# The second block's input units as three fp32r products each, with their split halves made on ScalarE and VectorE and one expert transfer issued later

## The chip, the cores and the metric

The program runs on one core of one Trainium2 chip. The metric is the device time of one execution in microseconds (us), the median of the runs shown. The core has TensorE (PE, with its weight loads as PEld), VectorE (DVE), ScalarE (ACT), GpSimd (POOL) and SyncE (SP, which here only issues transfers). "Granted clock" is the share of TensorE's full clock in a stretch.

## What is computed

The reference is two models in a row on 256 tokens of width 1024, all in fp32. The first block has two layers (three mixing branches and a feed-forward part); the second block has one layer with modulation from a vector c, differential attention with four heads, a pooling branch, and 32 experts of which each token uses two. Around the change only these lines matter:

```python
mod = jax.nn.silu(c) @ w_ada[l] + b_ada[l]
sh1, sc1, g1, sh2, sc2, g2 = jnp.split(mod, N_MOD, axis=-1)
h = rms_norm(x, norm1_g[l]) * (1.0 + sc1[:, None]) + sh1[:, None]
z = h @ w_in[l]
...
x = x + g1[:, None] * mix
...
y = hierarchical_moe(h, w_rg, b_rg, w_re, b_re, w_gate, w_up, w_down)
```

The changed part is `z = h @ w_in`: 1024 inputs to 2048 columns (query, key, value and pool input, 512 each).

## The kernel before

**Units and the ring.** All weights come from HBM as one stream of units of 1 MB (128 partitions x 2048 fp32). SP issues them in the order of the stream into a ring of four slots; unit n waits until unit n - 4 is done on PE (L868 to L870). A unit of w_in holds 256 output columns: eight chunks of 128 inputs. `gemm2` (L1352) multiplies it with `u`, the modulated input (eight chunks of 128 x 256), in 32 fp32 products of 128 x 128 by 128 x 256, into one of two banks, which ACT copies out (`win_read`, L2122).

**Split products.** The rest of the kernel multiplies large matrices as three fp32r products: ACT writes the high part of a unit (a copy to fp32r, L2064), DVE the low part (unit minus high part, L2735, in place in the ring), the input has a high and a low part too, and PE adds high x high, high x low and low x high (L1064, L1069). The eight input units of the second block are the exception: they are multiplied as they are.

**Order in the second block.** The order of each engine's work is written out by hand. Units in the stream are numbered from the block's start: 0 and 1 are the first pair of modulation units, the eight input units lie at 2, 3, 6, 7, 10, 13, 14, 15 (`WIN_AT`), pairs of modulation units between them, 20 to 23 are the output units, 24 is the router, and then 192 units of experts follow. On PE (L1472 to L1511): norms, the first pair, `win(0)`, `win(2)`, a turn for rope, a pair, `win(4)`, a turn for rope, `win(6)`, a pair, the values' turn, scores of head 0, `win(7)`, scores of head 1, a pair, `win(1)`, turn of the weights of head 0, a turn for rope, `win(3)`, values of head 0, turn of the weights of head 1, a turn for rope, `win(5)`. In the text these eight are units 1 to 8 in this order. After them come the rest of attention and pooling, two pairs, the output products (`out_products`, L1452), the router, and the experts.

On DVE the same stretch runs: `both_norms` (L2753, writes u; ACT's `modulate2`, L2099, then scales it chunk by chunk in place), `first_norm` (L2760, rescales h), the keeping of modulation columns, two rope steps (L2837, three instructions that wait for PE's turn), values, maxima and weights of head 0, maxima of head 1, `pool_means` (L2807), copy of the turned weights of head 0, a rope step, weights of head 1, its copy, a rope step. An engine takes its instructions in this order, and a wait holds up all behind it.

**Expert transfers ahead of time.** Expert units 0 to 21 have places of their own, and SP issues them between the ring's units as their places come free (L871 to L902). Units 2 to 6 go behind the ring units 5 to 9 (L875); unit 7, whose place is u, waits for the last input unit (L878). Later expert units need a place that an earlier one gave up: the next is issued when the first expert's first unit is done on PE (L904). The experts' products then run per expert: gate and up (L1674), turns, down (L1708), with transfers of two units at once.

## Time and profile before

| | us |
|---|---|
| runs before | 2069.06, 2069.35, 2070.88 |
| median | 2069.35 |
| the profiled execution | 2068.3 |
| its span (first to last instruction) | 2066.5 |
| PE busy | 1930.7 (93%) |
| DVE busy | 1265.8 (61%) |
| ACT busy | 923.8 (45%) |
| DMA queue of SP | 479.57 MB, 60.2% of 16 engines' span |

All times below are microseconds from the span's start of this execution, whose own time is 2068.3; the median of the runs is 1.05 more. The second block starts near 1486, its input units run from 1493 to 1565, and the experts from 1629 to the end. A busy PE is not PE at its peak: products overlap in the records. A line can be that of a helper that many places call.

### The profile page before, as it was taken

What the parts mean: (1) busy time and instruction counts of PE and PEld (TensorE: products, weight loads), DVE (VectorE), ACT (ScalarE), POOL (GpSimd) and SP (SyncE); (2) the same over time, 40 slices, a digit from 0 to 9 for tenths busy, and PEclk for the clock granted to TensorE, in tenths of its full rate; (3) what the DMA queues carried; (4) which work ended last, traced back from release to release, by engine and by line L of the source; (5) the groups of instructions that cost most, each with busy time, mean ns of one, the idle gap of its engine ahead of it and who ended that gap; (6) DMA issues with size and microseconds to landing.
All of it is one profiled execution on the core that took longest, in us unless ns stands there. A gap on an engine that the chain in (4) does not pass through costs nothing.

```text
span 2066.5 us, 46188 instructions
## 1 busy us (share of the span) xinstructions
PE 1930.7 (93%) x19900; PEld 1726.2 (84%) x19900; DVE 1265.8 (61%) x2069; ACT 923.8 (45%) x1100; POOL 31.4 (2%) x62
## 2 busy tenths in 40 slices
PE   8999999999999999999999999999999897777766
PEld 7998989999999999989899999999987664454444
DVE  6889887698787468898885896885543311111111
ACT  5555644674555455557365755554412210111101
POOL 0000000000000000000000000000000000000000
PEclk9999999999999999999999999999999998899898
DMA  6455434545455554554544454455787899999997
GB/s 242 175 214 184 182 147 163 204 144 187 181 184 191 193 184 174 199 210 157 183 154 172 176 184 165 183 184 199 277 328 282 344 428 428 428 428 429 428 429 313
DMA packets 60272, 498.92 MB, mean 241 GB/s; under 512 B 7152, under 2 KB 7280, under 8 KB 12240
## 3 DMA queue, kind: packets, MB, share of 16 engines
q1 hardware_dynamic: 54864, 479.57, 60.2%
q0 software_dynamic: 4384, 14.49, 2.1%
q8 instruction: 129, 2.11, 0.4%
q10 hardware_dynamic: 864, 2.49, 0.3%
q14 instruction: 31, 0.25, 0.0%
HBM read 495.38 MB, written 1.15 MB: 240 GB/s over the span
## 4 chain that ended last, share of the span: by engine, by line
PE 77%; DMA 17%; DVE 4%; ACT 1%; issue 1%; ACTq 0%; SPq 0%; DVEq 0%
PE bank L1064 34%; PE bank L1069 17%; DMA arena<-stream 15%; PE bank L1009 4%; PE bank L1674 3%; PE bank L1361 3%; PE bank L1052 2%; DMA ring<-stream 1%; PE bank L1057 1%; DVE ring_r L2735 1%; PE banks_by_token L1267 1%; PE banks_by_token L1236 1%; PE bank L1708 1%; PE bank L1653 1%; PE bank L1106 1%
## 5 line engine op out<-in xcount | busy, mean ns | idle before, releaser
L1069 PE MATMUL bank<-gh_and_scan_weights_high,ring_r 128*128 128x256 f32 x2368 | 308.3, 283 | 0.7 <-DVE ring_r L2735 0.7
L2735 DVE TENSOR_TENSOR ring_r<-ring,weights_and_u_split 128x2048 fp32r<-128x2048 f32 x108 | 247.1, 2289 | 85.4 <-ACT weights_and_u_split L2064 81.8
L1069 PEld LDWEIGHTS bank<-gh_and_scan_weights_high,ring_r 128*128 128x128 f32 x2368 | 294.8, 192 | 1.1 <-DVE ring_r L2735 1.1
L2064 ACT ACTIVATE weights_and_u_split<-ring 128x2048 fp32r<-128x2048 f32 x108 | 205.8, 1908 | 83.3 <-PE bank L1069 53.5
L3096 DVE COPY arena<-bank 128x128 f32<-128x128 f32 x32 | 9.3, 292 | 288.8 <-PE bank L1692 288.8
L1674 PE MATMUL bank<-arena 128*32 128x256 f32 x1504 | 109.7, 443 | 60.7 <-DMA arena<-stream 59.8
L2735 DVE TENSOR_TENSOR ring_r<-ring,hidden_and_weights_high 128x2048 fp32r<-128x2048 f32 x64 | 146.1, 2286 | 32.9 <-ACT hidden_and_weights_high L2064 32.8
L2248 ACT ACTIVATE arena<-bank 64x256 f32<-64x256 f32 x32 | 12.1, 378 | 318.0 <-PE bank L1674 318.0
L1674 PEld LDWEIGHTS bank<-arena 128*32 128x32 f32 x1504 | 54.8, 124 | 111.6 <-issue 52.3
L1064 PE MATMUL bank<-gh_and_scan_weights_high,weights_and_u_split 128*128 128x256 f32 x992 | 141.1, 285 | 1.6 <-ACT weights_and_u_split L2064 1.6
L2307 DVE SCALAR_TENSOR_TENSOR arena<-bank,par,arena 128x255 f32<-128x255 f32 (+1 forms) x272 | 111.3, 475 | 48.8 <-ACT arena L1857 48.6
L1064 PEld LDWEIGHTS bank<-gh_and_scan_weights_high,weights_and_u_split 128*128 128x128 f32 x992 | 127.8, 192 | 3.3 <-ACT weights_and_u_split L2064 2.0
L1868 ACT ACTIVATE arena<-bank 128x512 f32<-128x512 f32 x96 | 56.9, 595 | 160.9 <-PE bank L1069 158.0
L2064 ACT ACTIVATE hidden_and_weights_high<-ring 128x2048 fp32r<-128x2048 f32 x64 | 122.0, 1908 | 9.8 <-PE bank L1009 8.5
L1064 PE MATMUL bank<-gh_and_scan_weights_high,hidden_and_weights_high 128*128 128x256 f32 x864 | 123.6, 286 | 0.0
L1064 PE MATMUL bank<-u_r,weights_and_u_split 128*128 128x256 f32 x864 | 121.3, 283 | 0.0
L1064 PE MATMUL bank<-u_r,hidden_and_weights_high 128*128 128x256 f32 x864 | 121.3, 283 | 0.0
L1857 ACT ACTIVATE arena<-bank,par 128x256 f32<-128x256 f32 x112 | 57.1, 561 | 130.3 <-PE bank L1069 127.6
L1064 PEld LDWEIGHTS bank<-gh_and_scan_weights_high,hidden_and_weights_high 128*128 128x128 f32 x864 | 111.2, 191 | 4.9 <-issue 4.3
L1064 PEld LDWEIGHTS bank<-u_r,weights_and_u_split 128*128 128x128 f32 x864 | 111.5, 192 | 0.0
L1064 PEld LDWEIGHTS bank<-u_r,hidden_and_weights_high 128*128 128x128 f32 x864 | 111.4, 192 | 0.0
L1064 PE MATMUL bank<-hidden_low,weights_and_u_split 128*128 128x256 f32 x608 | 86.0, 283 | 0.0
(497 smaller groups left out, 3493.8 us busy)
## 6 DMA issues: line engine op xcount, KB each, us to landing
ring<-stream SPq DMA_DIRECT2D x267, 1024.0 KB, 4.8
arena<-stream SPq DMA_DIRECT2D x55, 2048.0 KB, 25.8
ring<-stream SPq DMA_DIRECT2D x26, 2048.0 KB, 26.7
arena<-stream SPq DMA_DIRECT2D x19, 1024.0 KB, 9.8
arena<-rows_scratch POOLq DMA_DIRECT2D x48, 256.0 KB, 4.2
place_of_rows<-stream SPq DMA_DIRECT2D x2, 1024.0 KB, 6.4
place_of_parameters<-stream SPq DMA_DIRECT2D x2, 1024.0 KB, 6.5
h<-x_d ACTq DMA_DIRECT2D x4, 256.0 KB, 4.6
```

The source lines that it names most:

```text
L1009: mm = pe.matmul(G[use % GBANKS][:, :], xx[:, 4 * late + k, i * P:(i + 1) * P], wx[:, k, :], start=(not late and part == k == 0), stop=(la ...
L1052: pe.matmul(bank[:, c * S:(c + 1) * S], ww[k][:, c * P:(c + 1) * P], yhi[k] if xhi is None else xhi[:, k, :], start=(c == part == k == 0), ...
L1057: mm = pe.matmul(bank[:, c * S:(c + 1) * S], whi[k][:, c * P:(c + 1) * P], xlo[:, k, :], start=False, stop=(k == KC - 1), skip_group_check ...
L1064: pe.matmul(bank[:, c * S:(c + 1) * S], whi[k][:, c * P:(c + 1) * P], yhi[k] if xx is None else xx[:, k, :], start=(sub == 0 and c == part ...
L1069: mm = pe.matmul(bank[:, c * S:(c + 1) * S], wlo[k][:, c * P:(c + 1) * P], yhi[k] if xhi is None else xhi[:, k, :], start=False, stop=(end ...
L1361: mm = pe.matmul(G[b][:, c * S:(c + 1) * S], w[:, k, c * P:(c + 1) * P], x[:, k, :], start=(k == 0), stop=(k == KC - 1))
L1674: mm = pe.matmul(G[0][g:g + 32, 0:S], xe[:, 2 * j + k, a * SLOTS:(a + 1) * SLOTS], w[k][:, g * 8:g * 8 + S], start=(j == k == 0), stop=(j ...
L1857: a = act.activation(arena[:, dst, :], bank[:, c * S:(c + 1) * S], ACT.Identity, scale=pc(wn, ch * width + width // 2), bias=pc(bn, ch))
L1868: act.activation(flat(at, 2), bank[:, :], func).then_inc(f.sem, 1)
L2064: act.activation(high(k), scan_high_or_low(k, ring[:, POS[k] % RING, :]), ACT.Copy).then_inc(whi_ok.sem, 1)
L2307: ins = stt(o, bank[:, c * S + lo + d:c * S + hi + d], pc(wn, chans[c] * width + j), o, ALU.mult, ALU.add)
L2735: tt(scan_high_or_low(k, ring_r[:, POS[k] % RING, :]), scan_high_or_low(k, w), high(k).bitcast(F32), ALU.subtract)\
```

## The change

Each of the eight input units becomes three passes of 16 fp32r products: high part of the unit x high part of u, low part x high part of u, high part x low part of u. Below, these passes are the first, middle and last third of a unit. The first third waits for ACT's high part, the middle third for DVE's low part, the last third of the first unit in effect for the low part of u. ACT writes the high parts (`win_high`) into two places in turn, 138 and 88; DVE makes the low parts in place in the ring (`win_low`), the high part of u in eight casts and its low part in one subtraction (`u_parts`). Place 88 was expert unit 5's, so that transfer is issued behind the last input unit, ahead of expert unit 7.

```diff
@@ SP
                 elif second and 5 <= early < E_EARLY + 3:
                     sp.wait_ge(h_new.sem, h_new.at(DEPTH, 0))
-                    expert_unit(early - 3)
+                    if early - 3 != 5:
+                        expert_unit(early - 3)
                 elif second and early == WIN_AT[-1] + RING:
                     sp.wait_ge(*done2(WIN_AT[-1]))
+                    expert_unit(5)
                     expert_unit(7)
@@ PE
-            def gemm2(m, x):
+            def gemm2(m):
                 b, before = use2(m)
-                pe.wait_ge(*landed2(m))
+                n = WIN_AT.index(m)
+                whi, wlo = (x.rearrange("p (k m) -> p k m", k=KC) for x in (flat_r(WIN_HI[n % 2], KC), ring_r[:, m % RING, :]))
+                pe.wait_ge(whi_ok.sem, whi_ok.at(DEPTH, n + 1))
                 pe.wait_ge(freed[b].sem, before)
...
+                for part, (w, x) in enumerate(((whi, chunks_r(UHI, KC)), (wlo, chunks_r(UHI, KC)), (whi, u_r))):
+                    if part == 1:
+                        pe.wait_ge(wlo_ok.sem, wlo_ok.at(DEPTH, n + 1))
+                    elif part == 2:
+                        pe.wait_ge(ulo_ok.sem, ulo_ok.at(DEPTH, 1))
+                    for c in range(2):
+                        for k in range(KC):
+                            if part == n == c == 0:
+                                pe.wait_ge(uhi_ok.sem, uhi_ok.at(DEPTH, k + 1))
...
@@ ACT
+            def win_high(n):
+                m = WIN_AT[n]
+                act.wait_ge(*landed2(m))
+                if n >= 2:
+                    act.wait_ge(*done2(WIN_AT[n - 2]))
+                act.activation(flat_r(WIN_HI[n % 2], KC), ring[:, m % RING, :], ACT.Copy).then_inc(whi_ok.sem, 1)
...
             norm2(1)
+            win_high(0)
             modulate2()
...
+            act.wait_ge(h_new.sem, h_new.at(DEPTH, 0))
+            win_high(1)
             win_read(0)
             win_read(2)
+            win_high(2)
             ada_read2(1)
+            win_high(3)
...
             win_read(7)
+            win_high(5)
...
@@ DVE
+            def u_parts():
+
+                for c in range(KC):
+                    dve.wait_ge(u_ready.sem, u_ready.at(DEPTH, c + 1))
+                    V.tensor_copy(flat_r(UHI + c, 1), u[:, c, :]).then_inc(uhi_ok.sem, 1)
+                win_low(0)
+                dve.wait_ge(uhi_ok.sem, uhi_ok.at(DEPTH, KC))
+                tt(u_r[:].rearrange("p c s -> p (c s)"), u[:].rearrange("p c s -> p (c s)"), flat_r(UHI, KC).bitcast(F32), ALU.subtract)\
+                    .then_inc(ulo_ok.sem, 1)
+
+            def win_low(n):
+
+                m = WIN_AT[n]
+                dve.wait_ge(whi_ok.sem, whi_ok.at(DEPTH, n + 1))
+                tt(ring_r[:, m % RING, :], ring[:, m % RING, :], flat_r(WIN_HI[n % 2], KC).bitcast(F32), ALU.subtract).then_inc(wlo_ok.sem, 1)
...
             both_norms()
+            u_parts()
             first_norm()
...
+            win_low(1)
...
             rope(0, 0)
+            win_low(2)
             rope(2, 1)
+            win_low(3)
             ada_keep2(1)
+            win_low(4)
             values_kept(0)
...
             ada_keep2(2)
+            win_low(5)
             maxima(1)
             pool_means()
             ada_keep2(3)
+            win_low(6)
             turned(0)
             rope(1, 2)
+            win_low(7)
             weights(1)
```

DVE from the writing of u to the second rope step, before (arena is the large working area, banks_by_token the banks that PE's turns go to):

```order
L2757 TENSOR_TENSOR u<-arena,rstd 128x512 x4
L2764 SCALAR_TENSOR_TENSOR h<-arena,rstd 128x256 x8
...
L2787 TENSOR_TENSOR mod<-bank,arena 128x4
...
L2843 TENSOR_TENSOR arena<-banks_by_token,arena 128x512
L2844 TENSOR_TENSOR arena<-arena 128x512
L2846 TENSOR_TENSOR arena<-arena 128x512
L2843 TENSOR_TENSOR arena<-banks_by_token,arena 128x512
```

And the same stretch in the changed kernel (L2799 is a low part, L2792 the low part of u):

```order
L2782 TENSOR_TENSOR u<-arena,rstd 128x512 x4
L2789 CAST u_high_and_scan_weights_high<-u 128x256 x8
L2799 TENSOR_TENSOR ring_r<-ring,u_high_and_scan_weights_high 128x2048
L2792 TENSOR_TENSOR u_r<-u,u_high_and_scan_weights_high 128x2048
L2805 SCALAR_TENSOR_TENSOR h<-arena,rstd 128x256 x8
...
L2828 TENSOR_TENSOR mod<-bank,arena 128x4
L2799 TENSOR_TENSOR ring_r<-ring,weights_and_u_split 128x2048
...
L2885 TENSOR_TENSOR arena<-banks_by_token,arena 128x512
L2886 TENSOR_TENSOR arena<-arena 128x512
L2888 TENSOR_TENSOR arena<-arena 128x512
L2799 TENSOR_TENSOR ring_r<-ring,u_high_and_scan_weights_high 128x2048
L2885 TENSOR_TENSOR arena<-banks_by_token,arena 128x512
```

The final norm of h now stands behind the casts and two subtractions, and between two rope steps stands the low part of a unit. Later on DVE, behind the pooling (its last two instructions are the first rows here), the changed kernel has:

```order
L2860 TENSOR_TENSOR arena<-arena 128x256
L2862 TENSOR_TENSOR arena<-arena 128x256
L2828 TENSOR_TENSOR mod<-bank,arena 128x4
L2799 TENSOR_TENSOR ring_r<-ring,u_high_and_scan_weights_high 128x2048
L2932 COPY arena<-bank 128x512
L2885 TENSOR_TENSOR arena<-banks_by_token,arena 128x512
L2886 TENSOR_TENSOR arena<-arena 128x512
L2888 TENSOR_TENSOR arena<-arena 128x512
L2799 TENSOR_TENSOR ring_r<-ring,weights_and_u_split 128x2048
L2915 RECIPROCAL small<-small 128x4
```

Two low parts stand between the pooling and the weights of head 1 (which begin with the reciprocal); before, the same rows stood there without the two L2799. On SP, from the seventh ring unit's neighbours to the output units, before:

```order
L870 DMA ring<-stream 128x2048
L866 DMA arena<-stream 128x2048
L870 DMA ring<-stream 128x2048
L866 DMA arena<-stream 128x2048
L870 DMA ring<-stream 128x2048 x10
L866 DMA u<-stream 128x2048
L870 DMA ring<-stream 128x2048 x4
```

and in the changed kernel (arena and u here are the places of expert units):

```order
L871 DMA ring<-stream 128x2048 x2
L867 DMA arena<-stream 128x2048
L871 DMA ring<-stream 128x2048 x10
L867 DMA arena<-stream 128x2048
L867 DMA u<-stream 128x2048
L871 DMA ring<-stream 128x2048 x4
```

One transfer to the arena moved from the early stretch to the place between the last two of the input block's ring transfers and the four output units, ahead of the transfer to u.

## Rows read from the trace of the kernel before

**Rows 1.** Chain of waits near the end: start us, us, what

```profile
1692.88 26.70 DMA arena<-stream
...
2015.38 27.25 DMA arena<-stream
```

**Rows 2.** The page's moved bytes, 40 equal slices of the span

```profile
GB/s 242 175 214 184 182 147 163 204 144 187 181 184 191 193 184 174 199 210 157 183 154 172 176 184 165 183 184 199 277 328 282 344 428 428 428 428 429 428 429 313
```

**Rows 3.** Five-us stretches: length, PE, PEld, DVE, ACT, POOL busy, PEclk, DMA, GB/s

```profile
1590.00:1595.00 5.00, 3.63 (x17) 3.22 (x18) 0.00 (x0) 4.13 (x6) 0.00 (x0) 1.00 0.99 416
...
1620.00:1625.00 5.00, 2.56 (x119) 2.37 (x122) 3.89 (x25) 2.52 (x6) 0.00 (x0) 0.78 0.93 351
1625.00:1630.00 5.00, 3.01 (x97) 2.43 (x92) 0.73 (x4) 2.97 (x9) 0.00 (x0) 0.84 0.11 46
```

**Rows 4.** Timeline of SP's issues: start us, us, queue, line, transfer

```profile
1565.60 0.43 SPq L866 DMA_DIRECT2D u<-stream  x1
...
1630.91 0.33 SPq L866 DMA_DIRECT2D place_of_rows<-stream  x1
```

**Rows 5.** Chain of waits through the input units (L1361) to the output units

```profile
1478.38 1.92 PE bank L1069 x16
...
1493.65 7.10 PE bank L1361 x32
...
1508.23 0.86 PE banks_by_token L1391 x4
...
1558.29 6.91 PE bank L1361 x32
...
1570.59 5.73 DMA ring<-stream
```

**Rows 6.** Page, costliest groups: busy us, mean ns of one, idle before and releaser

```profile
L2735 DVE TENSOR_TENSOR ring_r<-ring,weights_and_u_split 128x2048 fp32r<-128x2048 f32 x108 | 247.1, 2289 | 85.4 <-ACT weights_and_u_split L2064 81.8
...
L2064 ACT ACTIVATE weights_and_u_split<-ring 128x2048 fp32r<-128x2048 f32 x108 | 205.8, 1908 | 83.3 <-PE bank L1069 53.5
```

**Rows 7.** DVE's groups by line and form, one copy in SBUF

```profile
L2639 DVE COPY arena<-arena 128x512 f32<-128x512 f32 x8 | 3.1, 424 | 0.1
```

**Rows 8.** Timeline of ACT and DVE: start us, us, engine, line, operation

```profile
1490.53 0.42 ACT L2090 ACTIVATE rstd<-rstd 128x256 f32<-128x256 f32 x1
...
1491.71 4.04 ACT L2103 ACTIVATE u<-u,mod 128x256 f32<-128x256 f32 x8 [0.76 <-DVE u L2757]
...
1497.07 3.25 DVE L2764 SCALAR_TENSOR_TENSOR h<-arena,rstd 128x256 f32<-128x256 f32 x8 [3.59 <-ACT rstd L1878]
...
1509.13 0.69 DVE L2843 TENSOR_TENSOR arena<-banks_by_token,arena 128x512 f32<-128x512 f32 x1 [7.62 <-PE banks_by_token L1391]
...
1510.45 0.69 DVE L2846 TENSOR_TENSOR arena<-arena 128x512 f32<-128x512 f32 x1
...
1537.04 0.60 ACT L2126 ACTIVATE arena<-bank 128x512 f32<-128x512 f32 x1 [3.63 <-PE bank L1361]
...
1538.48 1.29 DVE L2860 TENSOR_REDUCE small<-banks_by_token 128x2 f32<-128x512 f32 x2 [0.87 <-PE banks_by_token L1413]
...
1539.88 0.69 DVE L2811 COPY arena<-arena 128x1024 f32<-128x1024 f32 x1
...
1547.01 0.42 DVE L2820 TENSOR_TENSOR arena<-arena 128x256 f32<-128x256 f32 x1
...
1548.38 0.69 DVE L2890 COPY arena<-bank 128x512 f32<-128x512 f32 x1 [0.39 <-PE bank L1426]
...
1551.30 0.18 DVE L2873 RECIPROCAL small<-small 128x4 f32<-128x4 f32 x1
...
1552.43 0.88 DVE L2882 SCALAR_TENSOR_TENSOR arena<-arena,small 128x256 f32<-128x256 f32 x2
```

**Rows 9.** DMA issues at 1565 to 1566: target, KB, us to landing

```profile
ring<-stream SPq DMA_DIRECT2D x1, 1024.0 KB, 4.7
u<-stream SPq DMA_DIRECT2D x1, 1024.0 KB, 6.9
```

More of the change, by code:

```diff
@@ L347, in program @@
         HALF_AT = 120
+        WIN_HI = (138, 88)
         def bank(i):
@@ L1350, in first_norm @@
                 mm.then_inc(ss_ready.sem, 1)
-            def gemm2(m, x):
+            def gemm2(m):
                 b, before = use2(m)
-                pe.wait_ge(*landed2(m))
+                n = WIN_AT.index(m)
+                whi, wlo = (x.rearrange("p (k m) -> p k m", k=KC) for x in (flat_r(WIN_HI[n % 2], KC), ring_r[:, m % RING, :]))
+                pe.wait_ge(whi_ok.sem, whi_ok.at(DEPTH, n + 1))
                 pe.wait_ge(freed[b].sem, before)
-                w = ring[:, m % RING, :].rearrange("p (k m) -> p k m", k=KC)
-                for c in range(2):
-                    for k in range(KC):
-                        if m == WIN_AT[0] and c == 0:
-                            pe.wait_ge(u_ready.sem, u_ready.at(DEPTH, k + 1))
-                        mm = pe.matmul(G[b][:, c * S:(c + 1) * S], w[:, k, c * P:(c + 1) * P], x[:, k, :],
-                                       start=(k == 0), stop=(k == KC - 1))
+                for part, (w, x) in enumerate(((whi, chunks_r(UHI, KC)), (wlo, chunks_r(UHI, KC)), (whi, u_r))):
[7 more added lines that the diff above has]
+                                pe.wait_ge(uhi_ok.sem, uhi_ok.at(DEPTH, k + 1))
+                            mm = pe.matmul(G[b][:, c * S:(c + 1) * S], w[:, k, c * P:(c + 1) * P], x[:, k, :],
+                                           start=(part == c == k == 0), stop=(part == 2 and k == KC - 1), skip_group_check=True)
                 mm.then_inc(unit_done.sem, 1)
@@ L1382, in win @@
             def win(j):
-                gemm2(win_unit(j), u)
+                gemm2(win_unit(j))
             def rope_turn(j):
@@ L2150, in _ @@
                 return
+            act.wait_ge(h_new.sem, h_new.at(DEPTH, 0))
+            win_high(1)
             win_read(0)
             win_read(2)
+            win_high(2)
             ada_read2(1)
+            win_high(3)
             win_read(4)
             win_read(6)
+            win_high(4)
             ada_read2(2)
@@ L2158, in _ @@
             win_read(7)
+            win_high(5)
             ada_read2(3)
             exps(1)
+            win_high(6)
             win_read(1)
+            win_high(7)
             win_read(3)
```

## The prediction

> **What bounds the kernel now.** I read the end first. In the chain of waits the last 350 us are mostly one kind of step, a transfer of two expert units of 26 to 27 us, with a few microseconds of products between [rows 1]; the page's line of moved bytes stands at 428 GB/s there [rows 2]. So the last part is bound by bytes, and its length is fixed once it runs. The second question is what starts it. By the table of short stretches DMA is nearly idle at 1625 to 1630 (0.11) [rows 3], and SP issues its next transfer at 1630.91 [rows 4]. That transfer waits for the first expert's first unit on PE: every other place is full. So whatever makes the first expert start later or earlier by x moves the end by x. Earlier, that is capped at the 6 us or so of this lull; later, there is no cap. The third view is the chain from 1493 to 1577 [rows 5]: the eight input units, the turns and small steps between them follow each other on PE without a wait. The last unit ends at 1565.20, and at 1570.59 the chain changes to the transfer of the first output unit, which lands at 1576.3. From there PE, ACT and PE again lead to the first expert. I therefore ask two things: when does the eighth unit end, and when does that output unit land?
>
> **What the change saves on PE.** A unit is 32 fp32 products, 7.10 us (6.91 for the last two) [rows 5]. Sixteen fp32r products of the same size take 1.92 us [rows 5], so 48 take 5.76: 1.34 us saved a unit (1.15 for the last two), 10.3 us in all if PE waits for nothing.
>
> **What it adds.** ACT gets eight high parts of 1.908 us, DVE eight low parts of 2.289 us [rows 6], DVE also eight casts of one chunk of u and a subtraction of all of u. For the cast no row exists; a copy of 512 columns takes 0.424 us [rows 7], so 256 lie between half and all of that, and I take 0.3: it is paced by ACT anyway, and only the last one shows. The subtraction has the size of a low part, 2.29. DVE and ACT take their instructions in order, and the order decides which of these are hidden. PE needs a unit's low part for its middle third, 1.92 us after the unit starts.
>
> *Unit 1.* ACT is free at 1490.95 [rows 8] and now first makes the high part, to 1492.86. The eight modulations (4.04) [rows 8] end at 1496.9 instead of 1495.75. The last cast ends near 1497.3, the low part at 1499.6, the low part of u at 1501.95, and only then comes PE's last third, to 1503.9. Before, the unit ended at 1500.75 [rows 5]: **3.1 later**, though the products are fewer.
>
> *Units 2 to 4.* DVE now does the 3.25 us of the final norm of h [rows 8] behind these: 1501.95 to 1505.2. Small steps reach 1505.6, the low part 1507.9. PE has done the first third of unit 2 by then and waits about 1.8 us; the other two thirds (3.84) end at 1511.75. Now a loop closes. DVE's next instructions are a rope step, which waits for PE's turn after unit 2, and the low part of unit 3 stands behind it. Turn 0.86 [rows 5], rope 2.0 (1509.13 to 1511.14) [rows 8], low part 2.29, two thirds 3.84: 9.0, with hand-overs 9.1. So unit 3 ends at 1520.85, and unit 4, behind the second rope step, at 1529.95. DVE's idle time during a unit, which could have hidden these low parts, lies on the wrong side of the rope step.
>
> *Units 5 and 6.* Some 3.5 us of other PE work, unchanged, stand ahead of unit 5, and its low part is ready in time: the unit takes its 5.76 and ends at 1539.25. Unit 6 doesn't wait either. Here 1.34 each is gained.
>
> *Units 7 and 8.* From the end of unit 5 DVE is the chain. ACT reads the bank (0.60) [rows 8] and makes the sixth high part, to 1541.8; DVE does its low part, to 1544.1, the maxima (1.4 from their start to the next step), to 1545.5, and the pooling of 7.55 us (1539.88 to 1547.43) [rows 8], to 1553.1. Then low part 2.29, copy 0.69, rope 2.0, low part 2.29, weights 2.0 (1551.30 to 1553.31) [rows 8]: 1562.4, with hand-overs 1562.5. PE waits some 2.7 us in unit 7 for the first of these low parts, and 2.2 us ahead of the turn of the second head's weights, which stands before unit 8. After that two turns (1.3) and 5.76: unit 8 ends at **1569.6, 4.4 later** than 1565.20. Overlaps of neighbouring DVE instructions could take 0.6 off this, the delay of each wake-up could add 0.5.
>
> *The moved transfer.* Expert unit 5 (1 MB) leaves a stretch in which no unit waits for its weights and now stands, with unit 7 behind it, ahead of the first output unit. Before, unit 7's transfer was issued at 1565.60 [rows 4] and landed 6.9 us later [rows 9], at 1572.5; the output unit was issued at 1570.59 and landed at 1576.3 [rows 5], 3.8 after it. So it already lay behind a transfer, and one more 1 MB at 428 GB/s [rows 2] is 2.45 us: the upper end. A landing without a queue takes 4.7 us [rows 9], so 1.0 of the output unit's 5.73 was queue or disturbance, and the queue could have had up to 1.35 us of room: at least 2.45 - 1.35 = 1.1 must show. I take **2.1**, near the upper end, as the transfers ran almost without a gap. PE has no other work to put there. SP itself issues the same number of transfers; its order else is unchanged, and POOL's queue is not touched.
>
> **The sum.** 4.4 + 2.1 = 6.5 us. Nothing behind takes it up: from 1576 to the first expert each step waits for the one before, the transfers there are issued by that chain, and the byte-bound rest starts with it. The profiled execution (2068.3, span 2066.5) would give 2074.8; the median of the runs shown is 1.05 above it, so **2075.9**. Its own bounds: 1.1 for the transfer and 0.6 of overlap give 2074.3; 2.45 and 0.5 of wake-ups give 2076.7. A measurement of this kernel tells 0.2% (4.1 us) from no change: up to 2073.5 is the same.
>
> **Rivals.**
>
> *The transfer is hidden.* If PE comes to the output units later anyway, or the queue has room, 2.1 falls away: 2073.8, just above the bound of the same. Against it: the chain passes through that landing already [rows 5].
>
> *PE's clock falls.* In this trace PE, busy for about half of 1620 to 1625, shows a granted clock of 0.78 there and 0.84 in the next five us [rows 3]; with 0.5 as the lower level that is 2.2 and 1.6 us at half clock. Unit 1 now has some 4 us in which PE runs eight short products as they come, and then waits; before unit 8 it waits 2.2 us. In unit 1 the loss is hidden behind DVE's queue; ahead of unit 8 about 3.5 us at half clock cost 1.7: 2077.6. Against it: from 1590 to 1595 PE was busy 3.63 of 5 us, and the clock stayed at 1.00 [rows 3]. The Trainium skill's TensorE: Matmul & The Clock Gate (HAM oscillation) tells of kernels whose waits between groups of products make the clock fall each time; by that rule this rival would be the usual case. The trace only half agrees, by the same two rows.
>
> *Faster.* If each low part were ready when its unit's first third ends, seven units would save 9.0 us (five of 1.34, two of 1.15), less 3.1 for unit 1 and 2.1 for the transfer: 3.8 faster, 2065.6; with the transfer hidden too, 2063.5. It is decided on DVE: the low part must come before the rope step, or the rope step must not have to wait for PE. For it: DVE has idle time in each unit. Against it: the order of DVE's instructions.
>
> *Half of the waits.* If units 2 to 4 wait as I say, but the second head's weights are done in time (2.2) and the wait in unit 7 shrinks, 2.2 to 4 us less: about 2072.7.
>
> **How the numbers follow.** Forecast 0.57, transfer hidden 0.13, clock 0.13, half of the waits 0.10, faster 0.07. The range leaves out the faster rival and the outer parts of the others: 2071.0 to 2078.0. Faster by over 0.2%: 0.07. Same: half of the waits, and half of "hidden": 0.16. Slower: 0.77.
>
> **What would show it.** A wait of PE for DVE ahead of the middle thirds of units 2, 4 and 7 of 2 to 3 us, and next to none in units 5, 6 and 8; unit 1 ends near 1503.9; PE waits some 2 us ahead of the second turn of weights; unit 8 ends near 1569.6; the first output unit lands some 13 us after that instead of 11; the DMA lull before the first expert is the old one, 6 to 7 us later. I am wrong if unit 8 ends before 1566, if the output unit lands 11 us after it, or if the lull swallows part of the delay.

## The result and the profile after

The changed kernel takes 2080.45 us (median of six runs, 2076.96 to 2083.49) where the kernel before takes 2068.72: a ratio of 1.0059, 95% interval 1.0048 to 1.0069. Two later sets of the same kernel gave 1.0054 (1.0040 to 1.0067) and 1.0045 (1.0034 to 1.0056). So the change costs 9 to 12 us. The direction was as predicted; the size was not: 6.5 us were forecast, and the range ended at 2078.0.

The profiled execution took 2077.46 us, span 2075.6, which is 9.1 more than the span of before. Its chain of waits (start us, us, what) from the second block's first norm on, where [rows 5] and [rows 1] answer to it:

```profile
1488.91 1.15 PE bank L1344 x4
...
1507.35 4.10 PE bank L1370 x32
...
1516.75 4.10 PE bank L1370 x32
...
1532.17 8.89 DMA ring<-stream
...
1541.09 1.92 ACT weights_and_u_split L2142
...
1543.03 2.29 DVE ring_r L2799
...
1554.27 2.20 DVE ring_r L2799
...
1559.02 2.29 DVE ring_r L2799
...
1564.81 5.75 PE bank L1370 x48
...
1575.96 8.21 DMA ring<-stream
...
1584.21 5.24 PE bank L1473 x16
...
1638.64 5.30 PE bank L1683 x64
...
1702.86 27.07 DMA arena<-stream
```

In [rows 5] the units follow each other on PE. Here DVE's low parts (L2799) and two landings stand between them. Unit 8 (x48) ends at 1570.56, 5.3 us later than before. The first output unit is issued at 1575.96 and lands 8.21 us later. The first group of output products (L1473) takes 5.24 us; sixteen products of the same shape, one group later in this chain, take 3.46, and the first group took 3.72 in the kernel before. PE's own timeline gives its waits in brackets:

```profile
1507.35 2.18 PE L1370 MATMUL bank<-gh_and_scan_weights_high,ring_r 128*128 128x256 f32 x16 [1.18 <-DVE ring_r L2799]
...
1516.75 2.18 PE L1370 MATMUL bank<-gh_and_scan_weights_high,ring_r 128*128 128x256 f32 x16 [0.47 <-DVE ring_r L2799]
...
1526.15 2.18 PE L1370 MATMUL bank<-gh_and_scan_weights_high,ring_r 128*128 128x256 f32 x16 [1.96 <-DVE ring_r L2799]
...
1584.21 5.24 PE L1473 MATMUL bank<-arena,ring 128*128 128x256 f32 x16 [3.31 <-DMA ring<-stream]
```

The stretches around that last wait, and the lull before the first expert (columns as in [rows 3]):

```profile
1555.00:1560.00 5.00, 3.48 (x16) 3.48 (x17) 4.93 (x6) 0.00 (x0) 0.00 (x0) 0.66 0.00 0
1580.00:1585.00 5.00, 1.22 (x34) 1.05 (x35) 2.15 (x8) 2.24 (x9) 0.00 (x0) 0.89 1.02 428
1585.00:1590.00 5.00, 5.00 (x22) 4.17 (x21) 0.08 (x1) 0.00 (x0) 0.00 (x0) 0.77 0.99 413
...
1635.00:1640.00 5.00, 2.03 (x32) 1.18 (x36) 0.58 (x2) 1.69 (x6) 0.00 (x0) 0.85 0.10 38
```

PE is busy 1.22 us of five, and in the next five its granted clock is 0.77 of 2.4 GHz, so close to half of that time runs at 1.2 GHz; the group is 1.5 us longer. The lull of DMA is the old one of [rows 3], ten us later.

To compare kernels I count from T, the start of the first product of the second block's first norm (1488.91 here). What comes before T is the same code in all kernels, and T itself varied from 1487.6 to 1491.4. The kernels in the table are introduced below; fillers are products whose results nobody uses, and "four units" is a kernel that splits only units 2 to 5. All numbers are us after T, each a difference of two starts or ends in the chain of that kernel's profile; the ratio is against the runs of before.

| kernel | unit 8 ends | first output products start, take | first expert | end | ratio (95%) |
|---|---|---|---|---|---|
| before (three profiles) | 76.3 | 87.5, 3.72 | 140.1 to 140.4 | 577.4 to 577.9 | 1 |
| changed | 81.65 | 95.3, 5.24 | 149.7 | 586.7 | 1.0059 (1.0048, 1.0069) |
| changed, second | 81.58 | 95.4, 5.25 | 149.8 | 587.3 | 1.0054 (1.0040, 1.0067) |
| changed, third | 81.39 | 95.0, 5.29 | 148.5 | 583.8 | 1.0045 (1.0034, 1.0056) |
| move alone | 76.3 | 90.2, 6.75 | 146.5 | 580.9 | 1.0025 (1.0015, 1.0036) |
| no move | 82.6 | 94.2, 5.38 | 148.4 | 585.6 | 1.0044 (1.0030, 1.0058) |
| fillers at five places | 83.7 | 97.1, 3.46 | 147.2 | 581.4 | 1.0017 (1.0008, 1.0026) |
| fillers at one place | 83.5 | 97.2, 3.72 | 150.0 | 587.6 | 1.0046 (1.0033, 1.0060) |
| low parts earlier | 79.6 | 93.2, 6.56 | 148.9 | 584.6 | 1.0036 (1.0024, 1.0048) |
| the same, transfers later | 79.0 | 92.6, 5.13 | 146.4 | 583.3 | 1.0024 (1.0015, 1.0033) |
| before, transfers later | 76.3 | 87.7, 3.72 | 140.3 | 577.9 | 0.9998 (0.9989, 1.0007) |
| four units | 76.8 | 87.1, 3.65 | 137.6 | 574.0 | 0.9983 (0.9974, 0.9992) |
| four units, transfers later | 72.0 | 82.4, 3.65 | 131.5 | 569.6 | 0.9947 (0.9933, 0.9961) |

Two further sets of the kernel before, taken like a changed one, gave 0.9994 (0.9984 to 1.0005) and 0.9986 (0.9976 to 0.9996), so a ratio is good to some 0.15%. The 0.9983 of four units lies hardly outside that; for this kernel the profile has to bear the reading too.

### The profile page after: what moved, and what is told of

Read it like the earlier page. It is cut to its first block, busy times and chain, and to the rows that moved or that the text cites. A ratio compares the mean times of both kernels' runs of the same rounds, so it can differ in the third digit from the quotient of the medians.

```text
span 2075.6 us, 46478 instructions
## 1 busy us (share of the span) xinstructions
PE 1928.8 (93%) x20028; PEld 1727.9 (83%) x20028; DVE 1287.8 (62%) x2086; ACT 938.2 (45%) x1108; POOL 31.5 (2%) x62
## 3 DMA queue, kind: packets, MB, share of 16 engines
HBM read 495.38 MB, written 1.15 MB: 239 GB/s over the span
## 4 chain that ended last, share of the span: by engine, by line
PE 73%; DMA 18%; DVE 7%; ACT 2%; issue 1%; ACTq 0%; SPq 0%; DVEq 0%
PE bank L1067 34%; PE bank L1072 17%; DMA arena<-stream 16%; PE bank L1012 4%; PE bank L1683 3%; PE bank L1055 2%; DMA ring<-stream 2%; DVE ring_r L2760 1%; PE bank L1060 1%; PE banks_by_token L1270 1%; PE bank L1370 1%; PE banks_by_token L1239 1%; DVE ring_r L2799 1%; PE banks_by_token L1318 1%; PE bank L1473 1%
## 5 line engine op out<-in xcount | busy, mean ns | idle before, releaser
L2332 DVE SCALAR_TENSOR_TENSOR arena<-bank,par,arena 128x255 f32<-128x255 f32 (+1 forms) x272 | 111.4, 476 | 48.8 <-ACT arena L1866 48.6
```

The source lines that it names most:

```text
L2332: ins = stt(o, bank[:, c * S + lo + d:c * S + hi + d], pc(wn, chans[c] * width + j), o, ALU.mult, ALU.add)
```

## The experiments

**The move alone, and the change without it.** `move_only` is the kernel before with one edit on SP; `no_move` is the changed kernel with the second place of the high parts at 106, so that expert unit 5 keeps its early place.

```diff
-                    expert_unit(early - 3)
+                    if early - 3 != 5:
+                        expert_unit(early - 3)
...
+                    expert_unit(5)
                     expert_unit(7)
```

> The kernel before with one part of the change: expert unit 5 is issued behind the last input unit, ahead of unit 7; the products stay fp32. If the move only adds queue to the first output unit, as the prediction has it, that unit lands 2.1 us later after unit 8 (13.2 us instead of 11.1) and the time rises by 2.1 to 2.5 us. If the longer wait of PE for that unit also makes its clock fall, as the profile of the changed kernel shows it, the first group of output products takes 5.2 us instead of 3.7, and the time rises by 3.6 to 4.0. If the transfer is hidden: within 0.5 us of before.

> The changed kernel without the move: the second place of the high parts lies elsewhere, and expert unit 5 is issued early, as before the change. Unit 8 should end as in the changed kernel, near 1570.5 (+5.3), and the first output unit land 11 us behind it. If the transfer cost its queue alone, this is 2.5 us faster than the changed kernel; if the wait for it costs the clock too, 4.0 us faster (+5.3 us over before in a profile, +5 to 8 by the medians). If the sixth unit's load is late for another reason than the queue of ring units, that stays.

The chain of `move_only`:

```profile
1569.35 8.38 DMA ring<-stream
...
1577.78 6.75 PE bank L1466 x16
...
1634.11 3.69 PE bank L1676 x64
```

Nothing but one transfer was moved, and the output unit lands 13.8 us after unit 8 instead of 11.1: 2.7 us, a little over the prediction's upper bound of 2.45. The wait for it costs the clock as well: the whole first group runs at half speed, 6.75 us, 3.0 more. That makes 5.6 at the end of this group. The first expert's products then ran at the full clock here (3.69 us, before: 5.38), which gave some of it back in this profile: 3.2 us at the end, 5.3 by the medians (2072.88 against 2067.6), where 3.6 to 4.0 were expected for the case that the clock falls too.

The chain of `no_move`:

```profile
1533.09 9.89 DMA ring<-stream
...
1577.87 6.13 DMA ring<-stream
...
1584.04 5.38 PE bank L1471 x16
```

The output unit lands 11.5 us after unit 8 again. But unit 8 ends 1.0 later than in the changed kernel, because unit 6's load now lands 9.89 us after its issue, not 8.89: expert unit 5's transfer is back ahead of it. And the clock falls here too, at a much shorter wait. The first output group in PE's timeline of this kernel and then of the kernel before:

```profile
1584.04 5.38 PE L1471 MATMUL bank<-arena,ring 128*128 128x256 f32 x16 [1.23 <-DMA ring<-stream]
```

```profile
1576.37 3.72 PE L1464 MATMUL bank<-arena,ring 128*128 128x256 f32 x16 [0.83 <-DMA ring<-stream]
```

PE waits 1.23 us here instead of the 3.31 of the changed kernel, and the group takes 5.38 us all the same; in the kernel before, after a wait of 0.83 us, it takes 3.72. So the length of that wait alone doesn't decide whether the clock falls.

The move buys 1.0 us at unit 8 and pays 2.1 at the output unit. By the profiles the change without it ends 1.1 and 1.7 us ahead of the changed kernel's first two, but 1.8 behind its third, in which the first expert ran at the full clock; by the medians of one set it is 2.0 us faster (2076.85 against 2078.81), not the 2.5 to 4.0 that I expected.

**PE's clock.** Two kernels with additional fp32r products whose results are used nowhere:

```diff
+            def keep_busy(n, bank):
+                x = chunks_r(UHI, KC)
+                for _ in range(n):
+                    pe.matmul(bank, x[:, 0, 0:P], x[:, 0, :], start=True, stop=True)
...
+                    if n == 0:
+                        pe.wait_ge(freed[n].sem, UB2 + 5)
+                        keep_busy(24, G[0][:, 0:S])
                     pe.wait_ge(*landed2(m))
```

`warm_out` has these 24 alone, ahead of the first output unit; `warm` has more of them ahead of the middle thirds of units 1, 2 and 4 and of the second turn of weights.

> The changed kernel with additional fp32r products in PE's waits, into banks that are free there; their results are used nowhere. They stand ahead of the middle thirds' waits of units 1, 2 and 4, ahead of the turn of the second head's weights, and ahead of the first output unit (24 of them). If PE's clock explains what the sum missed, the granted clock of 1584 to 1587 is 1.00 instead of 0.5 to 0.8, the first group of output products takes 3.7 us instead of 5.2, and the time falls by 1.5 us in a profile and by up to 4 by the medians. If the clock is not the cause, the additional products cost nothing or up to 1 us where they outlast a wait, and the first group stays at 5.2.

> The changed kernel with 24 additional fp32r products, their results unused, ahead of the first output unit alone. In the run with such products at five places the first group of output products ran at the full clock, but unit 8 ended 2 us later than in the changed kernel. If the clock at that place costs 1.5 us, unit 8 ends as in the changed kernel (81.6 us after the first norm's product), the first group takes 3.5 to 3.7 us instead of 5.2, and the time falls by 1.5 us at least, by more if the clock also stays up in the router's stage. If the earlier fillers did the work, the time stays at the changed kernel's, or falls by less than 1 us.

The chain of `warm`:

```profile
1584.98 3.07 PE bank L1358 x24
1588.05 3.46 PE bank L1484 x16
...
1638.09 3.56 PE bank L1694 x64
```

The fillers hold the clock: the output group takes 3.46 us. They outlast the waits, so it starts 1.8 later and ends where it ended without them, at T + 100.6. The gain comes behind: the first expert is reached 2.6 us earlier, and its products run at the full clock (3.56 us against 5.30). Together 5.3 to 5.9 against the first two profiles of the changed kernel (2.4 against the third, in which the clock stayed up there by itself), 7.5 by the medians (2071.31 against 2078.81), more than the 1.5 to 4 expected, and not at the place where I expected it.

The chain of `warm_out`, unit 4's middle third in PE's timeline, and the stretch around it:

```profile
1526.96 5.60 PE bank L1375 x32
...
1586.33 3.72 PE bank L1481 x16
```

```profile
1526.96 3.68 PE L1375 MATMUL bank<-gh_and_scan_weights_high,ring_r 128*128 128x256 f32 x16 [1.96 <-DVE ring_r L2807]
```

```profile
1525.00:1530.00 5.00, 3.04 (x14) 3.04 (x15) 1.98 (x2) 0.00 (x0) 0.00 (x0) 0.71 0.78 324
```

The output group is back at 3.72 us, so the price of the clock there, 1.5 us, is confirmed. The total isn't lower: in this execution the clock fell in unit 1 (0.64 at 1495 to 1500), which made units 2 to 4 start 0.6 later, and at unit 4's middle third (both later thirds 5.60 us against 4.10), and unit 8 ended 1.9 later. The expectation of an unchanged unit 8 was wrong. Unit 4's wait of 1.96 us is the one that the changed kernel has too, and there it cost no clock (2.18 us for the middle third). Unit 7's wait of 2.45 us is the mirror image: half clock behind it in the changed kernel, a middle third of 2.18 us behind it here and 2.17 in `no_move`. Whether a given wait drops the clock isn't the same in every execution, and these traces give no rule for it.

**Where the low parts stand.** `early_low` exchanges two pairs on DVE, shown here, and one on ACT (the third high part goes ahead of the read of unit 2):

```diff
+            win_low(2)
             rope(0, 0)
-            win_low(2)
+            win_low(3)
             rope(2, 1)
-            win_low(3)
```

`early_low_late` also issues expert units 4 and 6 later, behind ring units 15 and 18, where DMA idles.

> The changed kernel with two pairs of steps exchanged: DVE makes the low parts of units 3 and 4 ahead of the rope steps, not behind them, and ACT makes the third high part ahead of the read of unit 2. If the low parts of these units are late because they stand on the wrong side of the rope steps, units 3 and 4 lose 2.7 us each, unit 4 ends 40 us after the first norm's product at 1525 instead of 1530 (by the first profile's times), the load of unit 6 is issued as much earlier, unit 8 ends 5 to 5.5 us earlier, near 1565, and the time falls by 5 to 6 us, to within +4 to +6 of before. The rival: DVE, ACT or the load of the unit is the bound there anyhow, and the order is indifferent; then the ends of units 3 and 4 move by less than 1 us and the time stays within 1 us of the changed kernel.

> All eight units as fp32r products with the low parts of units 3 and 4 ahead of the rope steps, and expert units 4 and 6 issued behind ring units 15 and 18. In the kernel with that order alone unit 5's load landed 9.9 us after its issue, and PE waited for it. If the queue is the cause, the load lands some 5 us earlier, unit 5 ends 4 to 5 us earlier, unit 8 as much or, where DVE's chain from the pooling on holds it, 2 to 4 us earlier, and the time falls by 2 to 4.5 us below that kernel. If DVE's chain alone sets unit 8's end, the time doesn't move.

The chain of `early_low`:

```profile
1514.41 5.96 PE bank L1370 x48
...
1520.39 9.93 DMA ring<-stream
...
1582.36 6.56 PE bank L1473 x16
```

Unit 3 runs its 48 products without a wait now, and so does unit 4: the order was the reason for these waits. But they were 0.47 and 1.96 us, as the timeline above says, not the 2.7 each that I wrote; and then unit 5's load, issued when unit 3 ends, lands only 9.93 us later, and PE waits for it. Unit 8 ends 2.1 us earlier instead of 5, and so does the execution (584.6 against 586.7; by the ratios 2 to 5 us), where 5 to 6 were expected. With two transfers taken out of the way, unit 5 no longer waits, and the chain goes through unit 6's load instead (issued at 1531.49 there, landing after 9.21 us): unit 8 gains another 0.6 and the end 1.2, where 2 to 4.5 were expected.

One number holds through all of these: from the start of the sixth high part to the end of unit 8 the changed kernel takes 29.47 us (1541.09 to 1570.56), without the move 29.47, with the low parts earlier 29.46, with later transfers as well 29.45. This is DVE's chain of two low parts more, the pooling and the rope step. What a change ahead of it gains is what it gains at that high part.

**Only the units that can hide it.** `hybrid` makes units 2 to 5 from three products and leaves 1, 6, 7 and 8 in fp32, moves no transfer, and puts the low parts ahead of the rope steps. The low part of u has a place of its own, and DVE clears the margins of the pooling input later:

```diff
+        WIN_HI, WIN_ULO = (24, 138), 106
+        WIN_SPLIT = (1, 2, 3, 4)
...
+                if n not in WIN_SPLIT:
+                    pe.wait_ge(*landed2(m))
...
+                first_norm()
+                win_low(1)
```

`hybrid_late` also issues three expert units later:

```diff
-                elif second and 5 <= early < E_EARLY + 3:
+                elif second and early in (5, 6):
                     sp.wait_ge(h_new.sem, h_new.at(DEPTH, 0))
                     expert_unit(early - 3)
+                elif second and early in (15, 17, 18):
+                    expert_unit({15: 4, 17: 5, 18: 6}[early])
```

> Only units 2 to 5 as three fp32r products; units 1, 6, 7 and 8 stay fp32, no transfer is moved, the low parts stand ahead of the rope steps, and the low part of u has a place of its own. By the theory that the products save 1.34 us a unit and that only DVE's order, the eight casts ahead of unit 1 and the pooling take it away again, units 2 to 5 take 5.8 to 6.2 us each without waits of PE, unit 5 ends 4.5 to 5.4 us earlier than before, unit 8 as much earlier (near 1560.3 by before's times), the first output unit lands 11 us after it, and the time is 4 to 5.4 us below before. If the lull of the transfers ahead of the first expert is smaller than the 6 us read from before, or PE's clock falls at a further place, 1 to 3 us below. The rival: DVE's additional work delays the pooling, and PE waits ahead of the second turn of weights: no faster than before.

> The hybrid (units 2 to 5 as fp32r products, low parts ahead of the rope steps) with one more change: expert units 4, 5 and 6 are issued behind ring units 15, 17 and 18, in the stretch in which DMA idles, not at the time of unit 3. In the hybrid's profile unit 5 waited 3.3 us for its high part, since its load landed 12.0 us after its issue, and half clock then cost 1.6 us more; DMA was at 1.0 there for 20 us. If the queue of transfers is what took the hybrid's gain, that load lands 5 to 7 us after its issue, unit 5 takes 5.8 to 6 us instead of 7.45, unit 8 ends 71.5 to 72.5 us after the first norm's product (hybrid 76.75, before 76.3), and the time falls by 2.5 to 4 us below the hybrid, limited by the hybrid's smaller lull of DMA ahead of the first expert. If another thing holds unit 5's load, or the postponed transfers meet the output units, it stays within 1 us of the hybrid or is slower.

The chain of `hybrid` and two of its stretches:

```profile
1508.84 6.19 PE bank L1382 x48
...
1515.05 11.97 DMA ring<-stream
...
1529.01 7.45 PE bank L1382 x48
```

```profile
1520.00:1525.00 5.00, 5.00 (x59) 3.75 (x59) 0.00 (x0) 0.60 (x1) 0.00 (x0) 1.00 1.02 426
1525.00:1530.00 5.00, 1.71 (x12) 1.28 (x9) 1.01 (x1) 2.39 (x2) 0.00 (x0) 0.89 1.01 416
```

The expectation for unit 8 failed: it ends 0.4 later than before, not 5 earlier. Units 2 to 4 do take some 6 us, but unit 5's load lands 12 us after its issue while DMA is at its full 1.0; PE waits 3.3 us, and its clock falls (7.45 us instead of 5.95). The time is lower all the same, 4.2 us by the medians (2064.51 against 2068.72) and 3.4 to 3.9 in the profile: not through unit 8. The output unit has landed when PE comes to it, the first expert follows 46.9 us after the first output group instead of 48.8 to 49.2, and its products run at the full clock (3.69 us against 5.38). What these have to do with the four units is not shown.

The chain of `hybrid_late`, and the same stretch:

```profile
1516.77 5.95 PE bank L1384 x48
...
1526.23 5.94 PE bank L1384 x48
...
1570.77 3.65 PE bank L1487 x16
```

```profile
1520.00:1525.00 5.00, 5.00 (x59) 3.87 (x57) 0.00 (x0) 2.25 (x2) 0.00 (x0) 1.00 0.28 56
```

Now DMA has room (0.28), unit 5 doesn't wait, four units take 5.94 to 6.18 us instead of 7.10, and unit 8 ends 4.3 us earlier than before, at 72.0 as expected. With what follows that is 8.1 us in the profile, 9.2 by the medians (2059.69 against 2068.89), and a ratio of 0.9947. This version beats both kernels.

Whose gain is it, the products' or the later transfers'? `before_late` has the second of these two edits alone, in the kernel before.

> The kernel before, its products fp32 throughout, with expert units 4, 5 and 6 issued behind ring units 15, 17 and 18, as in the best kernel so far. If the four fp32r units make that kernel's gain and the queue of transfers only stood in their way, this one ends unit 8 at 76.3 us after the first norm's product as before, and stays within 1 us of before. If the transfers alone are worth part of it (the output unit and the router's weights land earlier, or PE's clock stays up ahead of the first expert), it gains 2 to 4 us without any fp32r product. If the postponed transfers meet the output unit, it is 1 to 2.5 us slower.

The same stretch of its profile:

```profile
1520.00:1525.00 5.00, 5.00 (x25) 4.41 (x24) 0.47 (x2) 0.00 (x0) 0.00 (x0) 1.00 0.32 133
```

DMA is as free as there (0.32; 1.01 in the kernel before), and nothing comes of it: unit 8 ends at 76.3, and the time is that of before (0.9998). The transfers are worth nothing by themselves. They are what the products' gain at unit 8 needs.

**The same kernels again.** Four further profiles of unaltered kernels, two of the changed one and two of the one before.

> The changed kernel unaltered, for a second profile and a wider set of times. If the part of its cost that lies beyond its profiled execution (+9.2 us there, +11.7 by the medians) is run to run, a second profile shows the same ends of the units within 0.5 us up to unit 8 (near 1570.5) and differs from the first only in stretches of half clock or in landings, each of which can be named. If it is a fixed cost that the first profile just missed, the second profile has one step that is 2 to 3 us longer and stays so in every further profile of a kernel that has this order.

> The changed kernel unaltered, a third profile. The medians put it 11 to 12 us above before, the profiles, counted from the first norm's product on, 9.1 and 9.7. In the traces so far the rest lies ahead of that product, at one load of the first block (issued near 246 us): it landed 4.8 to 5.1 us after its issue in four kernels with fp32 input units, and 5.2 to 6.7 us in six with fp32r units, and where it took over 6 us PE's clock fell behind it. If that is bound to the larger program, this profile has 5.2 us or more there; if it is chance, it may have 4.8. From the first norm's product to the end it takes 586.7 to 587.4 again in either case.

> The kernel before, unaltered, for a second profile. From the first product of the second block's first norm (at 1488.86 us in the first profile) to the end it took 577.6 us there; the two profiles of the changed kernel took 586.7 and 587.3 from the same product, though they reach it 2.5 us apart. If what lies ahead of that product is what moves from run to run, this profile gives 577.6 again within 0.7, and the first group of output products takes 3.7 us. If the first profile was a slow one for its kernel, as the medians (+11.2 to +11.7 us against +9.1 to +9.7 in the profiles) suggest, this one takes 575.5 to 576.5, and the stretch in which it is shorter shows a higher granted clock.

> The kernel before unaltered, a third profile, beside the one of the changed kernel. If the load near 246 us goes with the program, it lands 4.8 to 5.1 us after its issue again, and the first norm's product comes 1409.4 to 1409.8 us after the start of the loop of products at 79.5 us; if it is chance, it can be late here too. From that product to the end 577.6 to 577.9 in either case.

Counted from T, the kernel before repeats within 0.5 us. The changed one repeats to 0.1 us up to the first expert in two profiles; in the third the first expert's products ran at the full clock (3.69 us against 5.30), and it ended 3 us earlier, at 583.8, against the expectation of 586.7 to 587.4. T itself is late where one load of the first block is late. The chain of the second profile and a stretch behind it:

```profile
246.00 6.67 DMA ring<-stream
```

```profile
255.00:260.00 5.00, 4.31 (x92) 3.12 (x93) 4.60 (x4) 2.01 (x4) 0.00 (x0) 0.66 0.56 200
```

The same step in the third profile of the changed kernel:

```profile
245.93 4.76 DMA ring<-stream
```

So the load isn't late in every execution of the changed kernel, in code that the change doesn't touch; a late one is worth up to 3 us. That it is chance alone is not shown. Over all fifteen profiles the load took 4.79 to 5.17 us in the five kernels or repeats whose input units are all fp32, and 4.76 to 6.91 in the ten with split units, over 5.2 in eight of these. The larger program may make a late load more frequent, and that would be part of what the medians show and the profiles don't.

## Why the prediction was wrong, and where it was right

The forecast was 2075.9 and the median is 2080.45, 4.6 us more. The mechanism, direction and order of the steps held; what failed are terms of the sum. Three of them make the profile 9.1 us longer instead of 6.5: the start of the sixth high part, the moved transfer, and above all the clock, which the sum put at nothing. The fourth is the step from the profile to the median: the sum added the 1.05 of the kernel before, and the changed kernel's median lies 2.99 above its profiled execution. The cause of this last part, 1.9 us, is open.

**Right: what bounds the kernel, and the mechanism.** PE's gain of products is eaten by DVE's order. Unit 1 was put at 1503.9 and ended at 1503.63; unit 2 at 1511.75 (1511.45), unit 3 at 1520.85 (1520.85), unit 4 at 1529.95 (1530.24). That unit 3 fits to the hundredth is luck: unit 2 was 0.3 early, and the loop took 9.4 us instead of 9.1. The cast took 0.29 us (0.3 assumed). The lull of DMA swallowed next to nothing: the first output group ended 9.3 later, the first expert started 9.35 later, and the end came 9.1 later. The cap of about 6 us on a gain did not hold, though: four units with later transfers gained 8.1, and there the last transfer ahead of the lull, too, was issued 5.8 us earlier after T.

**Wrong: the start of the sixth high part, 0.9 us at unit 8.** The step on units 7 and 8 let ACT make it as soon as it had read the bank, from 1539.9. It began at 1541.09, 1.2 later. Unit 5 ended 0.45 late, at 1539.70, so that ACT had read the bank at 1540.33; then ACT waited 0.76 us for the unit's load, which was issued at 1532.17 and landed 8.89 us later, where [rows 9] show 4.7 without a queue:

```profile
1541.09 1.91 ACT L2142 ACTIVATE weights_and_u_split<-ring 128x2048 fp32r<-128x2048 f32 x1 [0.76 <-DMA ring<-stream]
```

From there the prediction's chain took 29.7 us to the end of unit 8, and the trace has 29.47. So the chain was right and its start was not: 5.3 us instead of 4.4. The sum asked when ACT and DVE are free and never asked whether the weights have landed. A split unit needs them earlier than an fp32 unit, by its high part (1.92 us), and DVE waits in order behind that.

**A little small: the moved transfer.** 13.6 us after unit 8 instead of 11.1: 2.5 where 2.1 was taken, at the upper bound, and 2.7 in the kernel with the move alone. That the transfer also helps unit 6's load (1.0 us) was not seen.

**Wrong: where the clock falls, 1.5 us.** The rival had the mechanism and the size (1.7), and put it ahead of unit 8. Near there the clock did fall (0.66 at 1555 to 1560), in unit 7's middle third behind a wait of 2.45 us, but DVE's chain hid it: the third took 3.69 us, and the wait of 2.2 us ahead of the turn of weights shrank to 0.31, while in `no_move` the third took 2.17, that wait 1.81, and the 29.47 us were the same. It cost 1.5 us where the sum had no entry: in the first output group, behind the 3.3 us for which PE waits for that unit. The prediction itself said that PE has nothing to put there, and that is the place to price the clock. At all seven waits of 3.3 to 3.5 us between 1490 and 1600 in these profiles, six at this place and one ahead of unit 5 in `hybrid`, the products behind took 1.4 to 3.0 us longer. Shorter waits went either way: 1.23 us at this place cost as much in `no_move` (5.38 us), and those of 1.96 and 2.45 us in units 4 and 7 cost clock in some profiles and none in others. The Trainium skill's TensorE: Matmul & The Clock Gate (HAM oscillation) describes a kernel in which each group of products waits for its transfer and then starts at half clock. The long waits here agree with it.

Unit 8, the transfer and the clock give 5.3 + 2.5 + 1.5 = 9.3 at the end of the first output group, and the profile measures 9.1 at its end; 4.4 + 2.1 + 0 were forecast.

**Open: the rest.** The medians lie 9 to 12 us above before. Of the scatter, two sources are shown: the load in the first block (up to 3 us, in eight of ten profiles with split units later than in any without) and the first expert's products at half or full clock (5.30 or 3.69 us). The slowest run of the changed kernel, 2084.90, is explained by no profile, and why its times scatter more (2073.61 to 2084.90) than those of before (2063.75 to 2072.95) is not shown.

**The rivals.** "Hidden" was wrong: the whole transfer showed. "Half of the waits" named a real change, as the wait ahead of the turn of weights all but went away (0.31), but PE filled it with products at half clock, and unit 8 came no earlier for it. "Faster" was named with the right condition, but its saving of 1.34 us a unit is 1.15 in the runs: 48 products take 5.95 us among the early units and 5.75 at the end, not 5.76 everywhere. And the condition on DVE is not enough: the loads have to be early as well, as the two kernels with four units show.

## What to carry to other kernels

Ask three things of a unit that is split into products of another type: when its low part is ready, when its weights have landed (it needs them earlier), and what PE's clock does at each wait that the new order leaves. Split only the units whose parts are hidden, and look at the queue of transfers as well as at the engines' order: with four units, taking three transfers out of a saturated stretch turned a gain of 4 us into 9; with all eight, the order gave 2.1 us at unit 8 and later transfers 0.6 more. Price a new wait of 3 us ahead of products at its length and 1.4 to 3.0 us of half clock, which is what the seven such waits here cost, and a shorter one as a risk with a chance.

## What the runs showed of the hardware

- A wait of PE of 3.3 us ahead of the output products made them 1.5 us longer (5.24 against 3.72); in the kernel with the move alone, behind 3.5 us, the whole group ran at half clock (6.75 against 3.46 at the full clock). A wait of 1.23 us at the same place in `no_move` cost as much (5.38), one of 0.83 us in the kernel before nothing. Twenty-four products without use in that wait brought the group back to 3.46 and 3.72 us.
- One queue of transfers of 1 MB: a load landed 4.7 us after its issue in an idle stretch [rows 9], 8.9 and 9.9 us behind others, 12.0 us where six transfers had been issued ahead of it within 10 us. The Trainium skill's DMA: Bandwidth & Descriptors (Queues, rings and completion order) says that on each DMA engine descriptors are consumed in ring order; the kernel with three of the transfers issued later is in keeping with that, as its load was there in time, though no run tells order apart from shared bandwidth. In the kernel before, the same three transfers moved changed nothing (0.9998).
- Not expected, and left open: between the first output group and the first expert the kernels take 48.2 to 49.6 us, but 45.5 to 47 in three of them (fillers at five places, four units, four units with later transfers). These are the kernels whose chain has no 7.4 us wait for a landing at the router's weights and less of what the profile calls issue ahead of the first expert.
